# Three norms between stages computed in column pieces, two norms merged into one, and the residual scaled later

## The reference, cut to what matters

```python
def hybrid_layer(x, ...):                 # first layer, 1024 tokens, width 1024
    ...
    x = x + mix @ w_out
    h2 = rmsnorm(x, norm2_g)              # the first of the three norms
    ff = square(relu(h2 @ w_up))          # 4096 wide
    return x + ff @ w_down
x = rmsnorm(hybrid_layer(x), final_g)     # the second ...
h_res = concatenate([meta, x])
for l in range(2):
    h = rmsnorm(h_res, norm_gain[l])      # ... with this one for l = 0; the third for l = 1
    proj = h @ w_in[l]                    # pool part u first, its gate z next
    y_pool = (pool_mix(u) * silu(z_pool)) @ pool_w_up[l]
    ...                                   # latent attention
    h_res = h_res + merged @ w_out[l]
```

## Time and profile before

| | us |
|---|---|
| median of 3 runs | 3325.3 (3324.19 to 3326.75) |
| the profiled execution, its own time | 3325.28 |
| its span, first to last instruction | 3323.5 |
| TensorE busy | 3054.6 (92%) |
| VectorE busy | 1412.9 (43%) |
| GpSimd busy | 1068.6 (32%) |
| ScalarE busy | 697.2 (21%) |

### The profile page before, as it was taken

The page is one execution under the profiler, slowest core; times in us unless marked ns, Lnnn a source line. Parts: engine busy times, 40 slices in busy tenths (PEclk is TensorE's granted clock), DMA queues, the critical chain, the costliest instruction groups (busy, mean ns, idle before and its releaser), DMA issues.

```text
span 3323.5 us, 41150 instructions
## 1 busy us (share of the span) xinstructions
PE 3054.6 (92%) x16352; PEld 2687.3 (81%) x16352; DVE 1412.9 (43%) x1726; ACT 697.2 (21%) x1241; POOL 1068.6 (32%) x1335
## 2 busy tenths in 40 slices
PE   6986687899999997799999899999899999899999
PEld 4764565777778775799999788889899999788889
DVE  4658454422222223820011666671820111666671
ACT  2142321000000002100111455510100111455510
POOL 3523013444444443333333211133433432211132
PEclk9997788999999998899999999999999999999999
DMA  2111011111111111211212100051211212000052
GB/s 105 44 32 35 1 70 37 47 50 44 44 50 44 44 50 38 82 47 45 96 51 78 38 14 14 14 181 51 90 51 45 97 46 83 33 14 14 14 187 77
DMA packets 46429, 182.50 MB, mean 55 GB/s; under 512 B 5968, under 2 KB 6096, under 8 KB 45776
## 3 DMA queue, kind: packets, MB, share of 16 engines
q1 hardware_dynamic: 31248, 113.19, 10.9%
q10 hardware_dynamic: 15040, 67.28, 5.3%
HBM read 150.06 MB, written 30.39 MB: 54 GB/s over the span
## 4 chain that ended last, share of the span: by engine, by line
PE 83%; DVE 12%; ACT 3%; issue 1%; DMA 0%; DVEq 0%; ACTq 0%; SPq 0%
PE acc L425 62%; PE acc L726 4%; PE aux L842 4%; PE acc L821 3%; DVE act_lo L1440 2%; PE acc L775 2%; PE acc L710 2%; DVE work L1456 1%; DVE work L1449 1%; DVE act_hi L1439 1%; PE acc L796 1%; DVE residual L1505 1%; PE acc L738 1%; PE acc L748 1%; PE acc L520 1%
## 5 line engine op out<-in xcount | busy, mean ns | idle before, releaser
L425 PE MATMUL acc<-act_hi,w_hi 128*128 128x348 f32 (+1 forms) x3104 | 768.7, 348 | 71.3 <-DVE act_lo L1440 36.0
L353 POOL TENSOR_TENSOR w_lo<-w_raw,w_hi 128x256 fp32r<-128x256 f32 (+1 forms) x924 | 810.4, 910 | 17.3
L425 PE MATMUL acc<-act_lo,w_hi 128*128 128x348 f32 (+1 forms) x3104 | 763.1, 346 | 0.0
L425 PEld LDWEIGHTS acc<-act_hi,w_hi 128*128 128x128 f32 x3104 | 545.2, 190 | 131.1 <-issue 52.6
L425 PE MATMUL acc<-act_hi,w_lo 128*128 128x348 f32 (+1 forms) x3104 | 616.7, 344 | 0.0
L425 PEld LDWEIGHTS acc<-act_lo,w_hi 128*128 128x128 f32 x3104 | 548.1, 190 | 43.3
L425 PEld LDWEIGHTS acc<-act_hi,w_lo 128*128 128x128 f32 x3104 | 527.7, 189 | 42.4
L373 POOL TENSOR_TENSOR small<-shape_consts 128x1 f32<-128x1 f32 x192 | 42.8, 223 | 1574.6 <-PE acc L425 1574.6
L425 PE MATMUL acc<-ff_split,w_hi 128*128 128x512 f32 (+1 forms) x1408 | 317.7, 375 | 12.0 <-DVE ff_split L1440 12.0
L1655 DVE TENSOR_TENSOR residual<-acc,residual 128x1024 f32<-128x1024 f32 (+1 forms) x88 | 108.1, 1228 | 460.0 <-PE acc L425 460.0
L425 PEld LDWEIGHTS acc<-ff_split,w_hi 128*128 128x128 f32 x1408 | 252.9, 188 | 61.0 <-DVE ff_split L1440 16.6
(11 more groups left out here) (228 smaller groups left out, 3288.4 us busy)
## 6 DMA issues: line engine op xcount, KB each, us to landing
w_raw<-in_wstream SPq DMA_DIRECT2D x215, 512.0 KB, 3.5
spill_x<-residual ACTq DMA_DIRECT2D x2, 4176.0 KB, 12.2
spill_m<-residual ACTq DMA_DIRECT2D x2, 4176.0 KB, 12.5
spill_g<-work ACTq DMA_DIRECT2D x16, 522.0 KB, 2.7
residual<-spill_m ACTq DMA_DIRECT2D x16, 522.0 KB, 6.1
work<-spill_g ACTq DMA_DIRECT2D x16, 522.0 KB, 8.9
residual<-spill_x ACTq DMA_DIRECT2D x16, 522.0 KB, 4.4
residual<-in_xT ACTq DMA_DIRECT2D x8, 512.0 KB, 9.8
```

The costliest lines, as they stand in the source:

```text
L353: ins = nc.gpsimd.tensor_tensor(Wl[:, s, c0:c0 + w], Wraw[:, s, c0:c0 + w], Wh[:, s, c0:c0 + w].bitcast(F32), ALU.subtract)
L425: ins = nc.tensor.matmul(acc[0:m, s, p, 0:w], wt[:, ws, w0 + j * m:w0 + j * m + m], x[:, k, p * w:p * w + w], start=(first and t == 0), st ...
```

## The change

**At each seam** the last two units of a stage (for the feed-forward part its last unit, which holds two result chunks) are worked through by column piece: piece 0 of both chunks, then piece 1, and so on (`close_two`, `close_down`). DVE and ACT add, square and total a piece when it is there, and TensorE slips the sum of a finished piece (`sum_piece`, into `aux`) between the products of the next. The opening pair of the next stage (`open_two`) takes piece 0 of all chunks first: four chunks of unit A with the hi weights, then their lo weights, the sum of the last piece, the other four chunks of A between the first products of unit B, B's lo weights, and then the further pieces for both units. The gained chunk (L1742 in the new kernel) is cast to hi by ACT instead of DVE.

**The merged norm** (second seam): a sum weighted by `final_g` squared gives one scale for `rmsnorm(rmsnorm(x, final), n2_0)`; the gain is the product of both. A second, unweighted sum (`plain`) is kept for the residual. The residual itself is scaled during the next layer: TensorE sums it after unit 2, ACT takes ln and exp, DVE multiplies the eight chunks, and ACT then sends eight DMAs to `spill_x` where there was one. The meta tokens get their own small norm. In the cut for this seam the pieces are 332, 348 and 344 columns.

**The angles and sines** are computed during `w_out` units 1 to 4 instead of after the norm.

```diff
+CUTS1 = (META, META + 512, T2)
+CUTS2 = (0, 348, 696, TP)
+CUTS_MID = (META, 348, 696, T2)
+        SPILL_ORDER = (2, 4, 5, 6, 7, 0, 1, 3)
+        SPILLED = (16 * KC, 16 * KC + 16)
+        NORM_ORDER = {
+            2: (("add", 0), ("norm", 0, 0, 4), ("add", 1), ("norm", 0, 4, 6), ("norm", 0, 6, 8), ("norm", 1, 0, 8)),
+            3: (("add", 0), ("norm", 0, 0, 3), ("add", 1), ("norm", 0, 3, 5), ("norm", 0, 5, 8), ("add", 2),
+                ("norm", 1, 0, 3), ("norm", 1, 3, 8), ("norm", 2, 0, 8)),
+        }
+        NORM_SCALE_AFTER = {2: (0, 3), 3: (0, 3, 6)}
...
+            def close_down(ws, cuts):
...
+                for p in range(n):
+                    a, b = cuts[p] - META, cuts[p + 1] - META
+                    for s in range(2):
+                        if p == 0:
+                            take(s)
+                        for k in range(FG):
+                            for t, (wt, x) in enumerate(pairs):
+                                ins = nc.tensor.matmul(acc[:, s, p, 0:b - a],
+                                                       wt[:, ws, s * 512 + k * P:s * 512 + k * P + P], x[:, k, a:b],
+                                                       start=(k == 0 and t == 0), stop=(k == FG - 1 and t == 2))
...
+                            if p and s == 1 and k == 1:
+                                sum_piece(p - 1, cuts)
+
+            def open_two(ws, pieces, cuts):
...
+                ahead = 4
...
+                begin(0, 0)
+                for k in range(ahead):
+                    arrived(0, k)
+                    piece_products(0, ws[0], 0, w, k, k == 0, False, (0, 1))
+                await_low()
+                for k in range(ahead):
+                    piece_products(0, ws[0], 0, w, k, False, False, (2,))
+                sum_piece(n - 1, cuts)
+                next_unit()
+                begin(0, 1)
+                for k in range(KC):
+                    if k + ahead < KC:
+                        arrived(0, k + ahead)
+                        piece_products(0, ws[0], 0, w, k + ahead, False, k + ahead == KC - 1)
+                    piece_products(1, ws[1], 0, w, k, k == 0, False, (0, 1))
+                await_low()
+                for k in range(KC):
+                    piece_products(1, ws[1], 0, w, k, False, k == KC - 1, (2,))
+                for p in range(1, n):
+                    for k in range(KC):
+                        for s in range(2):
...
-                norm_sum(0, PIECES2, R[:, 8, :])
-                wide_two(PIECES2, (sems["a_ready"], a_count), (ws(), ws()))
+                open_two((ws(), ws()), PIECES2, CUTS_MID if l == 0 else CUTS2)
                 for j in range(2, 8):
                     wide(j % 2, ws(), PIECES2)
-                a_count += 8
+                    if l == 0 and j == 2:
+                        pe.wait_ge(sems["x1_total"], 1)
...
+                            ins = nc.tensor.matmul(aux[:, p, :], ones, R[:, 16, CUTS1[p]:CUTS1[p + 1]],
+                                                   start=True, stop=True)
+                        ins.then_inc(sems["x1_summed"], 1)
...
                 for j in range(4):
                     await_unit(j % 2)
                     if j == 0:
                         by_signal(0)
                     release(copy(cut(R[:, j, 16:], PIECES2), acc_view(j % 2, PIECES2)), j % 2)
+                    if l == 0 and j == 1:
+                        residual_scale()
+                if l == 0:
+                    for i, j in enumerate(SPILL_ORDER):
+                        act.wait_ge(sems["x1_done"], i + 1)
+                        act.dma_start(spill_x[:, TP * j:TP * j + TP], X[:, j, :]).then_inc(sems["spilled"], 16)
...
+                if l == 0:
+                    norm_pieces(CUTS_MID, lambda j: S_[:, 8 + j:9 + j], down=True)
+                    do(vec.memset(R[:, 0:4, 0:16], 0.0), "to_act")
+                    for s in range(2):
+                        dve.wait_ge(sems["x1_squared"], s + 1)
+                        do(vec.tensor_tensor(R[:, 16, mid], R[:, 16, mid], R[:, 13 + s, mid], ALU.add),
+                           "x1_total" if s else "dve_step")
+                    dve.wait_ge(sems["x1_scale"], 1)
+                    for j in SPILL_ORDER:
+                        do(vec.scalar_tensor_tensor(X[:, j, mid], X[:, j, mid], param("final", j), R[:, 13, mid],
+                                                    ALU.mult, ALU.mult), "x1_done")
...
+                dve.wait_ge(sems["spilled"], SPILLED[l])
                 for g in range(4):
                     unit.step()
                     await_free(g % 2)
```

425 lines of the change are left out of this document (335 added, 90 removed).

## The result

| | before | after |
|---|---|---|
| median, us | 3325.5 (4 runs, 3324.19 to 3326.75) | 3277.1 (4 runs, 3275.92 to 3278.96) |
| ratio to before, 95% interval | | 0.9857 [0.9844, 0.9871] |
| profiled execution, its time / its span | 3325.28 / 3323.5 | 3276.70 / 3274.9 |
| mean granted clock of TensorE | 0.967 | 0.975 |

The change saves 48.4 us (1.4%); 51.8 were forecast, and 3277.1 lies in the range. First the two views that named the cause before, now of the changed kernel: the chain by engine, which answers to the earlier trace rows, and TensorE's waits, which answer to the earlier trace rows (L546 is the sum of a piece, L554 a product in an opening pair, L1735 the subtraction of a chunk, L2101 the z product, L659 the sum of the norm with which the program begins).

What follows compares the result with a forecast made beforehand. TensorE's work plus its waits for norms was taken as the bound. Seam gains 31.7 + 34.0 + 14.6, less 28.5, gave 51.8 off 3325.3: 3273 us, own range 3266 to 3281 (0.58), 8 in 10 3257 to 3291.

Steps and rivals of the forecast that it cites:

- first seam: From w_out to the next stage: remaining cost 8.0 us instead of 39.7, a gain of 31.7.
- second seam: Merged norm behind the feed-forward part: remaining cost 17.9 us instead of 51.9, a gain of 34.0.
- third seam: Last of the three stage changes: remaining cost 3.5 us instead of 18.1, a gain of 14.6.
- new wait and what goes with it: Layer after the second seam: TensorE waits 24.4 us for the first z product; with sums and restart, 28.5 lost.
- Signs that failed: Trace marks set beforehand: clock 1.00 in first and third seam, no sum wait above 6 us, no long 0.50.
- the adds have slack, no wait falls before the last sum: In the third seam, TensorE would not wait before the last sum; the seam's whole cost was put at 3.5 us.
- 0.2 for low parts: In the third seam's cost, the allowance for GpSimd's low weight parts: 0.2 us.
- The price of the angles without their cover: First seam: if units 1 to 3 fail to hide the angles, they cost at most their own 14 us.
- Third seam's spill and layer 1: Spill landing up to 8 us after the opening pair delays the mixing; costed at nothing, up to 5 us uncovered.
- Low clock to a losing extent: Rival: piecewise waits keep TensorE at 1.2 GHz through closing and opening pairs, 3398 us if throughout; chance 0.04.
- Late weights: Rival: opening pairs wait for their weights, 5 to 7 us per seam, 3290 us; chance 0.04.
- Dearer pieces: Rival: ScalarE-VectorE hand-overs 0.2 us dearer each, up to 13 us, or serial spills; 3281 to 3292 us, chance 0.15.

Runs made afterwards that it cites:

- Five spills: Against the changed kernel, layer 0's mixing waits only for the five residual spills of the chunks it overwrites, not all eight: 3273.1 us.
- no scaling: Against the changed kernel, the eight residual scalings are left out and the residual is spilled in one DMA after the last squares: 3252.3 us.
- mixing first: Against the changed kernel, the mixing uses work-area scratch and waits for neither scaling nor spill; scalings follow the second z product: 3252.7 us.
- High only: Against the changed kernel, GpSimd makes only 8 of the 1024 low weight columns of the six opening units: 3266.4 us.
- angles behind: Against the changed kernel, the angles and sines stand behind the first seam's norm again, positions still loaded early: 3291.7 us.

## Why the prediction held, and where it was off

Costs of the seams by the prediction's own marks, and what the trace after gives:

| | forecast | measured | the steps |
|---|---|---|---|
| first seam, cost | 8.0 | 10.0 | 602.0 - 520.0 = 82.0, less 72.0 |
| second seam | 17.9 | 19.3 | 53.4 - 34.1 |
| third seam | 3.5 | 7.8 | 53.7 - 45.9 |
| new wait and what goes with it | 28.5 | 27.3 | 107.1 - 79.8 |
| sum | 51.8 | 45.3 | 109.7 - 37.1 - 27.3 |
| gain of the spans | | 48.6 | 3323.5 - 3274.9 |

- **The new wait was right in nearly every step.** From E = 1316.2: unit 2 ended at 12.6 (12.2 forecast), the scale was there at 16.9 (16.4), the scalings ended at 28.3 (26.9), the last spill landed at 40.3 (38.8), the mixing ended at 71.5 (71.4), the wait was 24.0 (24.4). Two errors offset each other here: the last spill landed 1.5 late, and the mixing took 31.1 instead of 32.6. The restart cost 1.6, not 2.4. From the third unit to the product behind the mixing it is 1424.37 - 1317.27 = 107.1, before 1459.04 - 1379.23 = 79.8. Five spills, no scaling and mixing first each moved it by the amount expected.
- **Second seam.** Three waits of 3.5, 1.5 and 6.7, forecast 3.3, 3.0 and 5.4: together 11.6 against 11.7. It costs 1.4 more, since TensorE ran at low clock twice, after the first and the third wait, where I had counted one restart at 2.3 (its own numbers, 24.91 - 22.3, give 2.6). The first two of these windows of the changed kernel (columns as in the window above) show it; the third belongs to the third seam.

```profile
1274.00:1279.00 5.00, 4.94 (x15) 4.51 (x16) 2.17 (x5) 1.98 (x4) 0.00 (x0) 0.50 0.23 89
1290.00:1297.00 7.00, 4.07 (x14) 3.59 (x15) 6.41 (x13) 3.55 (x7) 0.00 (x0) 0.54 0.25 77
...
2299.00:2303.50 4.50, 4.50 (x19) 4.40 (x18) 4.21 (x8) 2.48 (x6) 1.09 (x2) 0.62 0.38 118
```

- **Signs that failed.** I had called myself wrong if TensorE showed 0.50 for more than 10 us in one seam. In the second it did: all 5.0 us of the first window and 6.4 of the 7.0 of the second (0.54 is the mean of 0.50 and 1.00), 11.4 together. It made the seam no more than 1.4 us dearer than forecast, since TensorE was waiting in part of it and one restart was in the sum. A granted clock of 1.00 in the first and third seam, and no wait for a sum above 6 us, did not come true either: 0.57 and 0.62, and 6.67.

- **The step that failed is "the adds have slack, no wait falls before the last sum" of the third seam**, with its 0.2 for low parts. GpSimd starts on the weights of both opening units just when VectorE is at the last chunks and the last total. Seven instructions of VectorE up to the total took 3.3 us longer together (0.79 of it one beside a cast), TensorE waited 2.65 and then ran at a granted clock of 0.62 (the last window above). The seam cost 4.3 more than forecast, most of the 6.5 us that the terms miss. High only shows the cause of the wait: it falls to 0.57, and the seam by 4.3. Some 1.5 of that is the low clock, which the same wait did not bring in five spills and angles behind; why it came in the one and not in the other is open. (The terms of this seam also add up to 3.6, not 3.5.)
- **First seam**: the same size is short. I counted 1.2 us of GpSimd for four chunks, and they took 9.2 instead of 7.2, where half of GpSimd's 3.2 is its two casts. Hence 0.56 and 0.84 of waits that I had not, and 2.0 instead of 1.3 at the sum. On the other side TensorE waited 1.3 for a chunk behind the sum, where I had 2.1 and 1.0. The price of the angles without their cover, "at most 14", is what angles behind measured: 14.6, nearly half of the 29.7 us that the seam gained.
- **Third seam's spill and layer 1**: costed at nothing, and nothing it is: from the third unit to the product behind the mixing 2402.64 - 2322.83 = 79.81, before 2449.32 - 2369.51 = 79.81.
- **What the terms don't hold**: 48.6 - 45.3 = 3.3 us. The kernel before ran 1.8 us longer in a stretch where both run the same instructions, shown here from the kernel before, and another 1.8 in the second layer's attention. Why is open; it isn't the change. By the terms alone the time would have been 3325.3 - 45.3 = 3280.0, so that 3277.1 comes this near to 3273 is partly luck.

```profile
1459.04 288.55 PE acc L425 x1800
...
2449.32 286.75 PE acc L425 x1800
```

- **The rivals.** Low clock to a losing extent did not happen: the clock was 0.50 to 0.62 in the three windows above and 0.57 from 552 to 556, and 1.00 from 556 to 602. Late weights: the closing pairs never waited for low parts, the opening one once, for 0.3 us; without the late order they would have cost 7.0. Dearer pieces: the seams cost 7.7 us more than forecast, but by GpSimd's work and the low clock, and no run tests that rival's dearer hand-overs; the time lies in my own range, below that rival's.

## What to carry to other kernels

When an engine's list gets new work between two stages, write the timeline from there to the next wait of the busiest engine: here it foretold a wait of 24 us to within 0.4, and it shows the cure, scratch space that doesn't wait for the work. Ask of each total, sum or scale which chunks stand ahead of it and whether the reader needs them yet; four chunks too many cost 3 us, none ahead cost 5. Where VectorE's chain sets a seam, count GpSimd's instructions beside it at their price for each one, casts included, over the whole chain; VectorE's adds from PSUM are free of it.
